# GpSimd's residual rows start behind a norm's last piece, the second half's transposes two jobs earlier, and the next weights are rounded behind the pieces

## What is computed

```python
# first block
u = layer_norm(x) * (1 + scale1) + shift1
x = layer_norm(a * x + gate1 * mixer(u), ln1_w, ln1_b)
u2 = layer_norm(x) * (1 + scale2) + shift2
x = layer_norm(a * x + gate2 * (square(relu(u2 @ w_ff1)) @ w_ff2), ln2_w, ln2_b)
# second block
h = layer_norm(a * x + mixer2(x), ln1_g, ln1_b)            # mixer2: z, SSD, S5, RG-LRU
h = layer_norm(a * h + cross_attention(h, mem), ln2_g, ln2_b)   # 4 heads, 256 memory rows
h = layer_norm(a * h + square(relu(h @ w1)) @ w2, ln3_g, ln3_b)
```

## Time and profile before

| | us |
|---|---|
| median of 3 runs | 3345.33 (3341.96 to 3348.39) |
| the profiled execution | 3340.57 |
| its span | 3338.8 |
| TensorE busy | 2724.1 (82%) |
| VectorE busy | 1622.2 (49%) |
| ScalarE busy | 967.5 (29%) |
| GpSimd busy | 816.4 (24%) |
| mean granted TensorE clock | 0.903 |

### The profile page before, as it was taken

How to read it: one execution, slowest core, us unless ns; L and a number is a source line. 1 busy time by engine, 2 the same in 40 slices (tenths; PEclk the granted TensorE clock), 3 DMA queues, 4 the chain that set the end, 5 groups by cost and what they waited for, 6 DMA issues and landing times.

```text
span 3338.8 us, 34230 instructions
## 1 busy us (share of the span) xinstructions
PE 2724.1 (82%) x13318; PEld 1407.7 (42%) x13318; DVE 1622.2 (49%) x2357; ACT 967.5 (29%) x1115; POOL 816.4 (24%) x258
## 2 busy tenths in 40 slices
PE   2789758786799999995968795675789599999997
PEld 1467545543344444442444442232344244444443
DVE  6544453248444444467354559947323722222225
ACT  2232222212422222223233253213232332222221
POOL 0533350010111111124121122414200511111114
PEclk9899866888899999997878897787899799999998
DMA  7222220020111111120021120011001011111111
GB/s 242 72 64 77 67 76 26 26 84 6 51 51 50 50 50 50 51 64 13 26 76 63 64 76 0 0 38 51 26 26 38 26 51 51 50 50 50 50 38 51
DMA packets 95597, 172.84 MB, mean 52 GB/s; under 512 B 5600, under 2 KB 37744, under 8 KB 94704
## 3 DMA queue, kind: packets, MB, share of 16 engines
q1 hardware_dynamic: 81072, 130.50, 12.1%
q10 hardware_dynamic: 14400, 40.65, 3.4%
HBM read 164.85 MB, written 6.29 MB: 51 GB/s over the span
## 4 chain that ended last, share of the span: by engine, by line
PE 64%; DVE 17%; DVEq 7%; ACT 4%; issue 4%; PEld 1%; POOLq 1%; DMA 1%; ACTq 1%; PEldq 0%; POOL 0%; SPq 0%
PE PS L582 19%; PE PS L583 19%; PE PS L584 19%; DVE XT L1841 3%; DVEq L1840 2%; ACT WS L1329 1%; PE PS L1262 1%; ACT WB L1328 1%; DVE S L2510 1%; DMA R<-in_x 1%; DVE S L2514 1%; PE PS L1235 1%; DVE ST L1860 1%; DVEq L2516 1%; DVE S L1904 1%
## 5 line engine op out<-in xcount | busy, mean ns | idle before, releaser
L458 POOL TENSOR_TENSOR WB<-WS,WB 128x2048 f16<-128x2048 f32 x108 | 447.8, 4168 | 2013.8 <-ACT WS L1329 2013.5
L582 PE MATMUL PS<-XT,WB 128*128 128x512 f16 (+1 forms) x1584 | 608.5, 384 | 80.6 <-DVE Hf L1839 29.9
L583 PE MATMUL PS<-XT,WB 128*128 128x512 f16 (+1 forms) x1584 | 607.7, 384 | 0.0
L584 PE MATMUL PS<-XT,WB 128*128 128x512 f16 (+1 forms) x1584 | 607.4, 383 | 0.0
L582 PE MATMUL PS<-WB,Hf 128*128 128x512 f16 x1440 | 549.9, 382 | 30.0 <-DVEq L1844 10.2
L583 PE MATMUL PS<-WB,Hf 128*128 128x512 f16 x1440 | 549.4, 382 | 0.0
L584 PE MATMUL PS<-WB,Hf 128*128 128x512 f16 x1440 | 549.0, 381 | 0.0
L1839 DVE CAST Hf<-S 128x512 f16<-128x512 f32 x172 | 124.8, 725 | 572.2 <-ACT S L1541 459.3
L1328 ACT ACTIVATE WB<-WS 128x2048 f16<-128x2048 f32 (+3 forms) x118 | 212.3, 1799 | 586.3 <-PEq L591 552.9
L582 PEld LDWEIGHTS PS<-XT,WB 128*128 128x128 f16 (+1 forms) x1584 | 156.3, 99 | 279.9 <-issue 60.4
L2141 DVE SCALAR_TENSOR_TENSOR R<-PS,R 128x512 f32<-128x512 f32 x176 | 120.9, 691 | 263.0 <-PE PS L584 258.5
(11 more groups left out here) (341 smaller groups left out, 3263.5 us busy)
## 6 DMA issues: line engine op xcount, KB each, us to landing
WS<-in_w_ff SPq DMA_DIRECT2D x32, 1024.0 KB, 5.0
WS<-in_mlp_w SPq DMA_DIRECT2D x32, 1024.0 KB, 5.2
Hf<-in_w_ada ACTq DMA_DIRECT2D x16, 1024.0 KB, 7.8
WS<-in_w_in SPq DMA_DIRECT2D x48, 256.0 KB, 4.2
Hf<-in_w_ada SPq DMA_DIRECT2D x8, 1024.0 KB, 10.8
WS<-in_w_out SPq DMA_DIRECT2D x8, 1024.0 KB, 5.1
WS<-in_w_in SPq DMA_DIRECT2D x14, 512.0 KB, 3.8
R<-in_x SPq DMA_DIRECT2D x1, 4096.0 KB, 14.2
```

Source lines behind the costliest of these rows:

```text
L458: pool.tensor_tensor(WB[:, slot, 1, hf * 2048:(hf + 1) * 2048], WS[:, hf, :], WB[:, slot, 0, hf * 2048:(hf + 1) * 2048], ALU.subtract).the ...
L582: pe.matmul(o, ah, bh, start=(first and k == 0), stop=False, skip_group_check=True)
L583: pe.matmul(o, ah, bl, start=False, stop=False, skip_group_check=True)
L584: mm = pe.matmul(o, al, bh, start=False, stop=(last and k == n - 1), skip_group_check=True)
```

## The change

It has five edits.

1. GpSimd's `residual` waits, ahead of its first tile, for all 16 transposed blocks and for the norm's last piece (`PIECES`: 128, 156 and 188 pieces since the start).
2. TensorE issues the second half's transposes after two jobs instead of four, in z, in the queries and in the second MLP. The first MLP keeps four.
3. ScalarE rounds the second chunk of the next stage behind the second half's pieces, for the three norms with `roots == 1`.
4. VectorE's wait for the residual in the second MLP stands inside the loop, behind the first eight hidden pieces of a round, ahead of its first down steps.
5. `mlp` has an argument `rest_at` for edit 2.

```diff
+        PIECES = {"mlp1": 128, "o2": 156, "wo": 188}
...
             def residual(tail, first, rows_at):
 
                 pool.wait_ge(ln_rows, tail + 1)
+                need_side_done(pool, SIDE[first] + 15)
+                pool.wait_ge(piece_done, PIECES[first])
                 for t in range(TT):
-                    if t % 4 == 0:
-                        need_side_done(pool, SIDE[first] + 2 * t + 7)
                     pool.tensor_tensor(R[:, t, :], R[:, t, :], S[:, rows_at, :], ALU.mult)
...
                 for j in range(8):
-                    if j == 4:
+                    if j == rest_at:
                         rest[0]()
...
-            mlp(C["mlp1"], lambda t: R[:, t, :], False)
+            mlp(C["mlp1"], lambda t: R[:, t, :], False, 4)
...
             for t in range(4):
+                if t == 2:
+                    rest[0]()
                 rows_gemm(XT, range(KT), t, (0, HALF), W)
-            rest[0]()
             pe.wait_ge(piece_done, pieces)
...
             for f in range(4):
+                if f == 2:
+                    rest[0]()
                 query_job(f // 2, f % 2, 0)
-            rest[0]()
             pe.wait_ge(piece_done, pieces)
...
-            mlp(C["mlp2"], None, True)
+            mlp(C["mlp2"], None, True, 2)
...
-                round_chunk(first + 1)
+                if roots == 2:
+                    round_chunk(first + 1)
                 columns_half(scale, bias)
+                if roots == 1:
+                    round_chunk(first + 1)
...
                 hidden(0, 0)
-                if last:
-                    dve.wait_ge(res_ready, 24)
                 with dve.Fori(0, 3) as i:
                     for u in range(2):
                         hidden((u + 1) % 2, 16 * i)
+                        if last and u == 0:
+                            dve.wait_ge(res_ready, 24)
                         down(48 * i, False)
```

More of the change, by code:

```diff
@@ L913, in _, with mlp @@
             pieces += 16
-            def mlp(c0, src, last):
+            def mlp(c0, src, last, rest_at):
                 def hidden_job(W, j, par, extra):
```

## The result

| | before | changed |
|---|---|---|
| median, us | 3345.26 (3341.96 to 3348.39, 4 runs) | 3229.5 (3228.15 to 3233.22, 4 runs) |
| ratio | | 0.9656, 95% interval 0.9639 to 0.9673 |
| span of the profiled execution | 3338.8 | 3226.4 |
| TensorE busy | 2724.1 (82%) | 2712.4 (84%) |
| VectorE busy | 1622.2 | 1587.9 |

The medians are 115.8 us apart and the two spans 112.4. TensorE's work is the same but for the slow matmuls, which the granted clock shows.

What follows compares the result with a forecast made beforehand. TensorE was taken as held at three norms, 133.4 us of gaps, by VectorE pieces slowed beside GpSimd's residual. Gains of 110.1 less 0.5, 8.7 and 4.1 made 96.8, against the median 3248 us; range 3231 to 3272.

Steps and rivals of the forecast that it cites:

- A, gap and slow matmuls: At z's norm: next job starts at 1558.2 instead of 1592.3, 34.1 us less, plus 2.7 from the clock.
- A, dt's split: After z's norm: dt's narrow split, queued behind the residual, makes TensorE wait; 0.5 us lost.
- B, gap and slow matmuls: At the queries' norm: next job starts at 2313.1 instead of 2347.7, 34.6 us less, plus 2.1 from the clock.
- B, attention: Head 0 of attention: residual and wo0's split slow VectorE's quarter scalings; 8.7 us lost, bounds 0 and 24.
- C, pacing and the held bank: Second MLP: slowed hidden pieces cost 0.7 us, next weights' split holds a bank 3.4; 4.1 lost, bounds 0 and 12.
- the rival that the change doesn't do what it says: At the three norms: pieces slow for another cause, only the transposes' shift gains; 3320 us, chance 0.02.
- the one that the pieces stay partly slow: At each norm: the rounded weights' split reaches the last pieces, up to 8.1 us lost; 3272 us, chance 0.06.
- The rival "slower": All three places: TensorE stands still for residual and the split behind it, 150 us against 110; 3385 us, chance 0.02.
- The bound of 0: Head 0 of attention: no loss, as ACT's rounding covers it, quarter 2 already waiting 12.6 us for ACT.
- the 2.8 behind the rounding: At z's norm: two DMA issues, a table load and the first evacuation follow ACT's rounding before bank 0 frees; 2.8 us.
- The upper rival: Attention and MLP pay more for the moved residual: 30 us more, 3278; half of it, 3263; chance 0.18.
- The rule of the Trainium skill: Attention quarters: would count the small tensor_scalar as blocked, 2.5 us more for each of three, time 7 us higher.

Runs made afterwards that it cites:

- e1: Kernel before with only GpSimd's residual made to wait for the norm's last piece; 3251.3 us, ratio 0.9731.
- e7: Changed kernel with the residual's two operations done twice at z's norm, and its signal a separate instruction; 3274.99 us, ratio 0.9804.
- e4: Changed kernel with the second half's transposes back behind four jobs; 3259.97 us, ratio 0.9757.
- e9: Changed kernel with dt's split behind the fourth residual tile, query transposes and rounding behind three jobs, four hidden evacuations before second-MLP rounding; 3225.85 us, ratio 0.9654.
- e5: Changed kernel without the residual's arithmetic at the queries' norm, signals kept; 3229.29 us, ratio 0.967.
- e6: Changed kernel without the residual's arithmetic at the second MLP's norm, signals kept; 3229.5 us, ratio 0.9676.
- e8: Changed kernel with the residual's two operations done twice at the second MLP's norm, and its signal a separate instruction; 3267.45 us, ratio 0.9772.
- e10: Changed kernel with VectorE's wait for all 24 residual rows back ahead of the last MLP's loop; 3237.63 us, ratio 0.9694.
- e11: Changed kernel run again unaltered, as yardstick; 3234.64 us, ratio 0.9687.
- e12: Changed kernel with the residual's two operations done twice at the queries' norm, and its signal a separate instruction; 3248.19 us, ratio 0.9724.

## Why the prediction was right in kind and wrong in size

Each part's own term, against the landmarks and the shifts of TensorE's timeline:

| step of the sum | forecast | measured |
|---|---|---|
| A, gap and slow matmuls | 34.1 + 2.7 | 38.3 |
| A, dt's split | -0.5 | -1.0 |
| B, gap and slow matmuls | 34.6 + 2.1 | 37.3 |
| B, attention | -8.7 | +0.4 |
| C, gap | 34.8 | 35.2 |
| C, slow matmuls | 1.8 | 1.8 |
| C, pacing and the held bank | -4.1 | 0.0 |
| between and ahead of the places | 0 | 0.4 |
| sum | 96.8 | 112.4 |

**Right**: that the residual made the pieces slow (e1, which moves the residual alone); pieces of 0.42 and 0.69 in all three second halves; the waits left at B and C (4.73, 2.80); no slow matmuls behind the gaps; dt's split as the one wait behind the residual. e1 rules out the rival that the change doesn't do what it says, and the rows of VectorE the one that the pieces stay partly slow. The rival "slower" has its condition met in e7: with 45 us more of GpSimd at A, TensorE stands still for 45.7. The cover there had been forecast at 43.6 us against 41 of residual, and it was short by 1.0.

**Wrong, first step: the attention.** The sum took 8.7 us for it, because "both halves of it hit quarter 3", and that is the step that failed. The changed kernel's quarter 3 begins 1.2 us ahead of the split, and the whole attention lost nothing (0.4 gained in place of 8.7 lost). I had also counted the three quarters beside the residual but not the collision that they replace, the 3.1 us of the split in the kernel before. The bound of 0 was the outcome, and I had named its reason (ScalarE's rounding covers quarter 2) and not taken it. e4 suggests that the mechanism exists: there the split starts 1.3 us ahead of the scaling instead of 1.2 behind it, and the way to the value products is 6.8 longer.

**Wrong, second step: the second MLP.** The pacing of 5.27 against 5.18 and the split that "holds one bank for 3.4" are in the trace (casts and subtracts of 4.29 and 4.38 behind 2594.05), but VectorE had the lead of one free subtract, 0.69 instead of 2.67 at 2556.77, and TensorE waited for nothing. The sum had 4.1 us here and the runs 0.0. VectorE's timeline of the changed kernel, then TensorE's of e7, whose work at C is that of the changed kernel:

```profile
2556.77 0.69 DVE L1847 TENSOR_TENSOR Hf<-S,Hf 128x512 f16<-128x512 f32 x1
...
2594.21 4.29 DVE L1845 CAST Hf<-S 128x512 f16<-128x512 f32 x1
```

```profile
2646.07 0.39 PE L589 MATMUL PS<-XT,WB 128*128 128x512 f16 x1 [3.41 <-DVE Hf L1851]
```

The cast ends at 2598.50, 0.30 us ahead of the matmul that needs it (2598.80). In e7 TensorE waits 3.41 for the same cast, and R is 3.8 longer. So the 3.4 can occur, and it was absent here by 0.3 us: luck of the phase, not cover that the forecast could have counted on.

**Wrong, third: tail A**, 1.5 us too little gained (36.8 forecast, 38.3 measured). Of the 2.8 behind the rounding, two DMA issues ran at 1546.60 beside ScalarE's work, and bank 0 was free when TensorE came to it.

These three and the small terms of the table make 15.6 us by the spans. The other 3.3 are in how the profiled executions stand to the medians: 4.7 below it before, 1.35 below it in the changed kernel. The range's lower end was the sum without any loss, plus a little clock luck, and it left no room for gains that were 2.5 us larger. The changed kernel beside e9 (0.9687) would have been inside it; the two ratios of the same kernel differ by 0.3%, so whether the time falls 1.5 us outside or just inside is chance; that the sum had 12.8 us of losses which did not come is not. The upper rival's terms also add up to 32 us, not to its 30.

**The rule of the Trainium skill** ("SBUF — State Buffer", SBUF: two separate sides), that a VectorE operation in a two-port mode and a GpSimd operation exclude each other for their whole length, had been set aside for the small tensor_scalar of each quarter, on the strength of a 128x1 row of 0.15. The rows bear the page out: the 128x2 one takes 1.34 or 1.35 beside the residual, 0.17 without it. The price it adds is nonetheless nothing in the sum, since e5 pays as much to the split.

## What to carry to other kernels

An operation on GpSimd isn't slow or fast for VectorE by its amount but by which VectorE operations it meets: the same 40 us cost some 30 a place in front of a norm's last pieces (e1 against before, 88.9 at three), and 1.0 at A, 0.2 and 0.1 at B and C behind them. When such work is moved, subtract the collision that it displaces, and ask by how much the cover holds or fails: here A had none left, C had 12 us ahead of the next split and 0.3 at one cast, and B was decided by 1.2 us. Parts that gain nothing one by one beside the wait (transposes forward, rounding behind) were worth 17 us together, since each needs the room that the other makes, and at C they were worth 0.4 until the moved wait of VectorE let them gain 6.0 more. Judge a schedule by TensorE's distance between landmarks, which repeated within 1 us, mostly within 0.02, where medians of the same kernel moved by 5.

## What the runs showed of the hardware

A tensor_scalar of 128x1 took 0.15 us beside a split; one of 128x2 took 1.35 beside the residual and 0.17 alone. Not every VectorE operation is held up: a reciprocal of 128x2 took 0.17 beside a split (2334.25 in e4), and a reduce of 128x512 took 0.69 beside the residual (2313.24 in the changed kernel). No run varied the width by itself.

The clock's answer to a short wait isn't fixed. In the changed kernel, e5, e6, e7, e8, e10 and e11 the wait of 2.80 at C is followed by full speed. In e12 the same wait, with TensorE's starts ahead of it the same to within 0.1 us for 60 us, is followed 1.5 us later by slow matmuls, with the granted clock at 0.66 from 2566.5 to 2570.0. TensorE's timeline of e12:

```profile
2564.43 0.38 PE L589 MATMUL PS<-XT,WB 128*128 128x512 f16 x1 [2.80 <-DVE Hf L1851]
...
2565.92 0.63 PE L589 MATMUL PS<-XT,WB 128*128 128x512 f16 x1
```

That is 1.5 us of the 5.5 by which R is longer there, and a wait of 2.06 for a cast, with 8 more slow matmuls, most of the rest. The phase of VectorE and GpSimd at C parts at one operation. In the changed kernel VectorE's subtract starts at 2556.77 and GpSimd's next row operation 0.09 us behind it; in e7 GpSimd's starts at 2600.06 and the subtract, 2.70 long, 0.20 behind that; e12 goes as e7. The form of the signal doesn't decide it, since e8 has it too and goes as the changed kernel. What does stays open.
